# A chunked delta-rule recurrence: four levels of a triangular inverse in 32-wide blocks, and two output blocks of an MLP interleaved

## The reference

```python
def step(state, inp):                       # for each token, 8 heads, state 64x64
    r_t, w_t, k_t, v_t, a_t, b_t = inp
    sa = jnp.einsum("bhvk,bhk->bhv", state, a_t)
    state = (state * w_t[:, :, None, :] + sa[..., None] * b_t[:, :, None, :]
             + v_t[..., None] * k_t[:, :, None, :])
    return state, jnp.einsum("bhvk,bhk->bhv", state, r_t)
...
def squared_relu_mlp(h, w_up, w_down):      # 1024 -> 4096 -> 1024
    return jnp.square(jax.nn.relu(h @ w_up)) @ w_down
```

## Time and profile before

| what | value |
|---|---|
| median of 3 runs | 2743.69 us (2730.34 to 2747.26) |
| the profiled execution | 2739.59 us |
| its span | 2737.8 us |
| mean granted TensorE clock | 0.979 of full |
| PE busy | 2587.3 us (95%) |
| chunks of the recurrence, first `u` to last `u` | 396.0 to 810.6 us |

### The profile page before, as it was taken

How to read it: one execution, slowest core, us unless ns; L and a number is a source line. 1 busy time by engine, 2 the same in 40 slices (tenths; PEclk the granted TensorE clock), 3 DMA queues, 4 the chain that set the end, 5 groups by cost and what they waited for, 6 DMA issues and landing times.

```text
span 2737.8 us, 34644 instructions
## 1 busy us (share of the span) xinstructions
PE 2587.3 (95%) x13906; PEld 2140.4 (78%) x13906; DVE 1136.0 (41%) x1331; ACT 696.1 (25%) x1053; POOL 320.1 (12%) x242
## 2 busy tenths in 40 slices
PE   6999899898989999999999999977999999999998
PEld 5888688787887788888888878744778888888887
DVE  3344466666643333323333343277333332333332
ACT  4010134433321211211122122265231121112212
POOL 0000033332323200000000040043310000000000
PEclk8999999999989999999999999999999999999999
DMA  3221000000011111111111111100111111111112
GB/s 109 79 60 52 15 1 1 2 1 2 13 35 52 41 47 47 54 46 46 47 52 46 46 41 54 31 1 0 42 44 47 47 54 46 46 46 53 46 46 77
DMA packets 166311, 110.54 MB, mean 40 GB/s; under 512 B 3582, under 2 KB 163668, under 8 KB 166228
## 3 DMA queue, kind: packets, MB, share of 16 engines
q1 hardware_dynamic: 163756, 100.39, 12.3%
q0 software_dynamic: 2416, 8.91, 1.0%
q10 hardware_dynamic: 56, 0.01, 0.0%
HBM read 102.49 MB, written 6.29 MB: 40 GB/s over the span
## 4 chain that ended last, share of the span: by engine, by line
PE 83%; DVE 9%; ACT 4%; issue 3%; DVEq 0%; DMA 0%; POOL 0%; SPq 0%; ACTq 0%; POOLq 0%
PE ps L261 70%; PE ps L958 1%; PE ps L1368 1%; PE ps L961 1%; PE ps L947 1%; DVE probs L1396 1%; DVE softmax_stats L1401 1%; PE ps L913 1%; DVE mlp_lo L450 1%; DVE stage L447 1%; PE ps L975 1%; ACT stage L423 1%; PE ps L895 1%; ACT mlp_hi L425 1%; DVE x_level L1059 1%
## 5 line engine op out<-in xcount | busy, mean ns | idle before, releaser
L261 PE MATMUL ps<-h_hi,w_hi 128*128 128x512 f32 x1856 | 579.2, 393 | 23.3 <-DVE h_lo L1706 10.1
L261 PE MATMUL ps<-h_lo,w_hi 128*128 128x512 f32 x1856 | 575.6, 391 | 0.0
L261 PE MATMUL ps<-h_hi,w_lo 128*128 128x512 f32 x1856 | 574.3, 391 | 0.0
L222 ACT CAST w_hi<-w_raw 128x1024 fp32r<-128x1024 f32 x180 | 189.3, 1052 | 966.1 <-PE ps L261 966.1
L261 PEld LDWEIGHTS ps<-h_hi,w_hi 128*128 128x128 f32 x1856 | 347.8, 189 | 98.4 <-issue 14.8
L261 PEld LDWEIGHTS ps<-h_lo,w_hi 128*128 128x128 f32 x1856 | 350.8, 189 | 74.0
L261 PEld LDWEIGHTS ps<-h_hi,w_lo 128*128 128x128 f32 x1856 | 350.6, 189 | 73.8
L261 PE MATMUL ps<-mlp_hi,w_hi 128*128 128x512 f32 x1024 | 317.7, 391 | 10.7 <-DVE mlp_lo L450 10.7
L261 PE MATMUL ps<-mlp_lo,w_hi 128*128 128x512 f32 x1024 | 315.5, 389 | 0.0
L261 PE MATMUL ps<-mlp_hi,w_lo 128*128 128x512 f32 x1024 | 315.4, 389 | 0.0
L455 DVE TENSOR_TENSOR residual<-residual,ps 128x1024 f32<-128x1024 f32 x128 | 156.2, 1220 | 355.8 <-PE ps L261 355.8
(11 more groups left out here) (249 smaller groups left out, 2451.3 us busy)
## 6 DMA issues: line engine op xcount, KB each, us to landing
w_raw<-in_mlp_up SPq DMA_DIRECT2D x64, 512.0 KB, 4.0
w_raw<-in_mlp_down SPq DMA_DIRECT2D x64, 512.0 KB, 3.4
w_raw<-in_w_in_ab SPq DMA_DIRECT2D x26, 512.0 KB, 3.9
w_raw<-in_w_qkv SPq DMA_DIRECT2D x10, 512.0 KB, 3.9
x_in_tile<-in_x POOLq DMA_DIRECT2D x8, 512.0 KB, 4.2
w_raw<-in_w_out_ab SPq DMA_DIRECT2D x8, 512.0 KB, 4.1
w_raw<-in_w_o SPq DMA_DIRECT2D x8, 512.0 KB, 3.9
out<-out_chunk SPq DMA_DIRECT2D x8, 512.0 KB, 3.2
```

Source lines behind the costliest of these rows:

```text
L222: nc.scalar.copy(WH[:, slot], WR[:, slot]).then_inc(w_hi, 1)
L261: m = nc.tensor.matmul(acc(a_slot, half), ww, xx[:, k, half * HALF:(half + 1) * HALF], start=first, stop=last)
```

## The change

The first four levels keep only the 32x32 diagonal blocks, packed side by side in tiles of 128x256 (`TIC`, its transpose `TTC`, `YLC`, `MTC`). A product of a level becomes 32 matmuls of 32x32: all eight heads of diagonal tile 0, then of tile 1, and so on. There is one y and one dt for all heads, no dtt: DVE transposes the 32x32 blocks (`TTC` from `TIC`), at the start too, where this takes the place of PE's transposes and ACT's copies. POOL first copies the four diagonal quarters of `MTRB` to `MTC`, then makes `TTC`, then all four masked `XLC`; after level 3 it copies `TTC` to the diagonal of `TIT` for level 5, and ACT copies two quarters to `TI5`. DVE now waits for POOL's `tt` between the masks m and n. In the MLP the first two output blocks are interleaved.

```diff
+        def diag_products(ps, left, right):
+            for q in range(4):
+                for h in range(8):
+                    m = nc.tensor.matmul(ps[quarter(q), h], left[quarter(q), h], right[quarter(q), h],
+                                         start=True, stop=True)
+            return m
+
+        def diag_levels(t, c, s, prep, outp):
+            T, MM = solve_pe, nc.tensor.matmul
+            for k in range(MASKED):
+                solve_pool.wait(t, c, f"x{k}")
+                solve_dve.wait(t, c, f"t{k - 1}" if k else "ti")
+                T.done(diag_products(block_bank(2, 32), XLC[:, k], TIC), f"y{k}")
+                if k == 0:
+                    solve_dve.wait(t, c, "n1")
...
+                    T.done(m, "nv")
+                if outp:
+                    out_pe_step(t, c - 1, k)
+                if prep:
+                    prep_pe_step(t, c + 1, 1 - s, k)
+                solve_act.wait(t, c, f"y{k}")
+                if k:
+                    solve_dve.wait(t, c, f"tt{k - 1}")
+                T.done(diag_products(block_bank(3, 32), TTC, YLC), f"dt{k}")
...
         def chunk_act(act, c, s, prep, outp):
-            solve_pe.wait(act, c, "t0_0")
-            T.done(nc.scalar.copy(heads(TI, 0), bank(0)), "t0_0")
...
+                if k < MASKED:
+                    solve_pe.wait(act, c, f"y{k}")
+                    T.done(nc.scalar.copy(YLC[:, :], block_bank(2, 32)[:, 0:8]), f"y{k}")
+                elif k == 4:
+                    solve_dve.wait(act, c, "t3")
+                    nc.scalar.copy(TI5[quarter(0), :, 0:32], TIC[quarter(0)])
+                    T.done(nc.scalar.copy(TI5[quarter(1), :, 32:RH], TIC[quarter(1)]), "half")
...
         def chunk_dve(dve, c, s, prep, outp):
+                    solve_pool.wait(dve, c, "tt")
+                    T.done(nc.vector.transpose(TIC[:, :], TTC[:, :]), "ti")
-            for b in two:
-                T.done(TT(heads(XL, b), MTRB[:, 4 * b:4 * b + 4, 0], over(CON[:, C_MX:C_MX + P], 4), ALU.mult),
-                       f"x0_{b}")
...
+            for k in range(MASKED):
+                solve_pe.wait(dve, c, f"dt{k}")
+                T.done(TT(TIC[:, :], TIC[:, :], block_bank(3, 32)[:, 0:8], ALU.add), f"t{k}")
+                T.wait(dve, c, f"t{k}")
+                T.done(nc.vector.transpose(TTC[:, :], TIC[:, :]), f"tt{k}")
+                places(k)
...
         def chunk_pool(pool, c, s, prep, outp):
+            solve_dve.wait(pool, c, "m1")
+            for q in range(4):
+                T.done(nc.gpsimd.tensor_copy(MTC[quarter(q)], MTRB[quarter(q), :, 0, quarter(q)]), f"mc{q}")
+            T.done(TT(TTC[:, :], MTC[:, :], diag_const(C_M0), ALU.mult), "i")
+            T.done(TT(TTC[:, :], TTC[:, :], diag_const(C_I32), ALU.add), "tt")
+            for k in range(MASKED):
+                T.done(TT(XLC[:, k], MTC[:, :], diag_const(C_MX + 32 * k), ALU.mult), f"x{k}")
+            for k in range(LEVELS):
+                if k == 4:
+                    solve_dve.wait(pool, c, "tt3")
+                    for q in range(4):
+                        T.done(nc.gpsimd.tensor_copy(TIT[quarter(q), :, quarter(q)], TTC[quarter(q)]), f"full{q}")
...
         def mlp_pe(t, l):
+            def first_pair(g, after):
+                for n, (m, k) in enumerate(((0, 0), (0, 1), (0, 2), (1, 0), (1, 1), (0, 3), (1, 2), (1, 3))):
+                    if n < 3 or k == 3:
+                        t.wait_ge(act_lo, 4 * NG * l + 4 * g + 2 + k)
+                    if n == 3:
+                        t.wait_ge(acc_free[1], a0_ // 2 + 6 * g + 3)
+                    for ww, xx in ((w_h, ACh), (w_h, ACl), (w_l, ACh)):
...
+                first_pair(g, after)
+                for m in range(2, 8):
```

More of the change, by code:

```diff
@@ L295, in group @@
                             between=between if j == 0 else None)
-                for m in range(8):
+                first_pair(g, after)
+                for m in range(2, 8):
                     product(t, m // 2 % 2, m % 2, a0_ // 2 + 6 * g + 2 + m // 2, u0 + 8 * g + 4 + m // 2,
[L298 to L301, removed]
+                            GF, 256, P * (m % 2), ACh, ACl, new_unit=m % 2 == 0,
+                            between={2: lambda m=m: after(t, m - 1)} if after else None)
             group(0, norm_between(t, f"mlp{l}"))
@@ L857, in quarter_blocks @@
                 waited(t, "pe")
+                if b == 0:
+                    for h in range(8):
+                        m = MM(block_bank(1, 32)[low, h], TTC[low, h], YLC[low, h], start=True, stop=True)
+                    T.done(m, "dt4")
                 for h in range(8):
[L859 to L862, removed]
+                    m = MM(block_bank(3 * b + 2, 32)[top, h], YLC[low, h], TTC[low, h], start=True, stop=True)
                 T.done(m, f"dtt4_{b}")
@@ L867, in half_blocks @@
             top, low = slice(0, RH), slice(RH, P)
-            solve_dve.wait(t, c, "t4_0")
+            solve_dve.wait(t, c, "t4")
+            solve_act.wait(t, c, "half")
             waited(t, "pe")
@@ L879, in half_blocks @@
             solve_dve.wait(t, c, "tt4_1")
+            solve_pool.wait(t, c, "full3")
             for b in two:
@@ L918, in chunk_pe @@
                     prep_pe_step(t, c + 1, 1 - s, HEAD[1])
-            for b in two:
[L920 to L962, removed]
+            diag_levels(t, c, s, prep, outp)
+            quarter_blocks(t, c, s, prep, outp)
+            half_blocks(t, c, s, prep, outp)
             for p in range(4):
@@ L1042, in chunk_dve, with places @@
             T, TT = solve_dve, nc.vector.tensor_tensor
+            def places(k):
+                for b in two:
+                    if outp:
+                        out_dve_step(dve, c - 1, 1 - s, (k, b))
+                    if prep:
+                        prep_dve_step(dve, c + 1, 1 - s, (k, b))
             if prep:
@@ new lines, in chunk_dve @@
+            for k in range(MASKED):
[4 more added lines that the diff above has]
+                places(k)
+            q0, q1, q2, q3 = (quarter(i) for i in range(4))
+            solve_pe.wait(dve, c, "dt4")
+            T.done(nc.vector.tensor_copy(TI5[q1, :, 0:32], block_bank(1, 32)[q1, 0:8]), "t4")
@@ new lines, in chunk_dve @@
+            solve_pe.wait(dve, c, "dtt4_0")
+            T.done(nc.vector.tensor_copy(TIT[q0, :, q1], block_bank(2, 32)[q0, 0:8]), "tt4_0")
+            solve_pe.wait(dve, c, "dtt4_1")
+            T.done(nc.vector.tensor_copy(TIT[q2, :, q3], block_bank(5, 32)[q2, 0:8]), "tt4_1")
+            places(4)
+            for b in two:
+                solve_pe.wait(dve, c, f"dtt5_{b}")
+                T.done(nc.vector.tensor_copy(TIT[0:RH, 4 * b:4 * b + 4, RH:P],
+                                             block_bank(3 * b + 2, RH)[0:RH, 0:4]), f"tt5_{b}")
@@ L1090, in chunk_dve @@
+            places(5)
             solve_pe.wait(dve, c, "u")
@@ L1099, in chunk_pool, with diag_const @@
             T, TT = solve_pool, nc.gpsimd.tensor_tensor
+            def diag_const(col):
+                return over(CON[:, col:col + 32], 8)
             if prep:
```

158 lines of the change are left out of this document (83 added, 75 removed).

## The result

The changed kernel takes 2824.36 us (median of 4 runs, 2811.19 to 2829.03), the kernel before 2737.02 us on the same chip, 87 us less. The recorded ratio is 1.0297, 95% interval 1.0263 to 1.0331, that is 72 to 91 us with 81 in the middle. The ratios given are the recorded ones; they can differ by a few thousandths from the quotient of two medians, and where the text counts by ratios, it counts by these. The profiled execution took 2824.97 us, its span is 2822.8 us.

A forecast was written before the change was run, and what follows sets the result against it. PE, busy 95% of the span, was taken as the bound. To 2739.6 us it added 112 (eight chunks at +14: clock +17.5, gain 3.5), took 10 for the MLP, and added 4 to the median: 2846 us, range 2750 to 2900.

The forecast's parts named there:

- PE bounds, and an edit counts by PE's queue: Whole kernel: PE busy 95% of the span; an edit counts by PE's queue or a handover PE waits for.
- MLP, -10: MLP: interleaved output blocks remove PE's 16 waits for the last hidden block, 0.67 us each; -10 us in sum.
- A new product 1.8 us at full clock: Levels: 64 instructions at 0.0275 us each, 1.8 us, the same as an old product of eight heads.
- The head loses 1 us: Start of the levels: y0 earlier, but nv and ACT's square later behind POOL's copies and DVE's wait; 1 us lost.
- Levels at full clock, -3.5 us a chunk: Recurrence: saved third products and transposes, less open handovers, net -3.5 us a chunk, -28 for eight.
- The clock falls near y0 and comes back in the tail or behind L785 and L686: Recurrence, each chunk: clock falls near y0, returning in the tail or for a while after L785 and L686.
- Two thirds of 31 us of work low: PE's work from y0 to L981's end: 20.5 of 31 us low, less 3 hidden, +17.5 us a chunk.
- 32-wide blocks double at low, 3.7 us a product: Levels: 32-wide products take some 3.7 us at 0.50 against 1.9 at 1.00, taken from 64-wide rows.
- the second rival: Levels: a low clock doesn't slow 32-wide blocks; +3 us a chunk, 2758 us in all; chance 0.09.
- The sum: Whole kernel: +14 us a chunk, +112 for eight, MLP -10, 2842; with 4 to the median 2846 us.
- What holds the clock is work on the full array; small blocks count for little: PE's clock: full-array work holds it, small blocks count for little, like idle time.
- Fast rival, 2706: Recurrence: the clock holds, or falls only here and there, giving 2706 us; chance 0.15.

The follow-up runs named there:

- fill_full: The changed kernel plus eleven discarded 128x128 by 512-column products a chunk, ahead of y0 and behind each y and dt; 2801.84 us, ratio to before 1.0267.
- rec_alone: The changed kernel with the MLP's old loop, so the recurrence part alone; 2842.75 us, ratio to before 1.0407.
- fill_small: The changed kernel plus discarded products of 16 blocks of 32x32, three ahead of y0, one behind each y and dt; 2884.17 us, ratio to before 1.0543.
- turn_fill: The changed kernel with the four diagonal tiles taken in turn and eleven discarded full-array products a chunk; 2703.54 us, ratio to before 0.9904.
- turn_head: The changed kernel with diagonal tiles in turn, masks n0, n1 before DVE's wait for tt, and nv ahead of y0; 2715.07 us, ratio to before 0.9932.

## Why the prediction was right

The forecast was 2846 us, and 2824 came. The sign and the mechanism were right: small blocks let the clock fall, and the low clock outweighs the work saved. Of its signs all came but the 3.7 us of a product at 0.50: the clock low for 307 of the 430 us from 400 to 830, a period of 70.7 us, PE idle 3.12 us ahead of y0 by POOL, no wait on `mlp_lo`. Two terms were off in size, the MLP and the small blocks at the low clock, and one, the levels at full clock, was never measured.

- *PE bounds, and an edit counts by PE's queue*: right, 91% of the chain.
- *MLP, -10*: the wait went as said, but it was worth 15.6 us (87.04 for 88.01 us a group, 16 times). The mis-sized term is the 0.67 us a wait; 0.97 was gained. I read the matmuls' wait where the weight loads' one, 1.1 us each, bounds it from the other side.
- *A new product 1.8 us at full clock*: 1.88 with its tail. The row of 32 instructions (L847) from which I took it has this same neighbour order, and I took 27.5 ns as the cost of a small block. It is the cost of a small block behind one on the same quarter. In turn a block's instruction costs 0.75 us / 64, some 12 ns. The forecast was right only because the kernel has the order of the row. For the old product the pair that I read (L958, L961) has eight instructions in 0.99 us, so 1.98 for sixteen and not 1.8: this term of the saving was if anything too small. By the Trainium skill ("TensorE: Matmul & The Clock Gate", "Wait — 56ns, not 53.3ns?") 25 ns is the floor however small the matmul; the 12 ns here contradict it for blocks on different quarters.
- *The head loses 1 us*: not readable, since the clock falls as `nv` starts, but its parts are. y0 4.5 us behind the masks m was forecast, 4.6 came (m ends at 494.34, y0 at 498.94). PE idle 3.1 us ahead of it, by POOL, as forecast. The copies were 0.44 us each for 0.53, the products 0.72 for 0.64, the transpose 0.45 for 0.42, a handover 0.60 to 0.65 for 0.5 to 0.6.
- *Levels at full clock, -3.5 us a chunk*: not shown. No run held the clock in the order of the changed kernel; fill_full came nearest, with 208.6 us low, and its best chunks took 61.4 us with 13.7 low and eleven fillers in them, against 59.2 before.
- *The clock falls near y0 and comes back in the tail or behind L785 and L686*: just so in chunk 2, at 500.9 and 541.9. In half of the chunks the low stretch is longer, 51 to 58 us, and ends in the tail.
- *Two thirds of 31 us of work low*: this is 20.5 us of work, which doubled is 41 us low a chunk. 51 us came between the first and the last `u`: more than two thirds.
- *32-wide blocks double at low, 3.7 us a product*: 3.03, by 1.6. This term was too dear, six or seven products a chunk by 0.65 us, and the longer low time took back most of it. With the assumed -3.5, the clock costs 15.0 us a chunk (70.7 - 59.2 + 3.5), against 17.5 forecast. An estimate from the rows of chunk 2 has this size too: seven products 1.15 us longer each than the first, `nv` 1.7, L811 0.9 and L712 0.9 longer than the same shapes at 1.00 make 11.5 us, and this chunk's period grew by 9.7 (58.2 to 67.9). That they slow hardly at all, the second rival, is not so.
- *The sum*: the recurrence was forecast at +112, rec_alone gave +112 and the changed kernel's profile +99 up to the last `u`; that the first number agrees to the unit is luck, as the terms above show. Seven chunks give 80 of the 99, 11.5 each for 14 forecast; 18.4 come ahead of the first `u`, which I had counted as one more chunk.
- *What holds the clock is work on the full array; small blocks count for little*: shown, by fill_small against fill_full, for small blocks of 32x32 with 32 columns; which of these measures counts is not parted. The rule of the Trainium skill that I weighed ("TensorE: Matmul & The Clock Gate", Part 1: the clock falls after idle windows) does not cover it: 40.45 of 40.50 us busy at a clock of 0.56, with the fall behind 5 us without a gap.
- *Fast rival, 2706*: it didn't happen, since the clock fell. turn_fill, with the tiles in turn and full-array fillers, took 2703.5 and was low for 93 us; that this is near 2706 is chance, since its products cost less than the rival's.

## What to carry to other kernels

Packing a computation into small blocks saves multiplications, but here a product of small blocks takes PE hardly less time (1.88 us for 2.04), and it puts at risk a clock that everything around it needs: look up the granted clock over the stretch, and try real or discarded full-array matmuls where PE would wait. When several small blocks lie on different quarters of the array, walk over the quarters in the inner loop; the order alone was worth 73 us here. And when an engine waits for a slow neighbour, look at what stands behind the wait (n0, n1 and `nv` here), and let it pass.

## What the runs showed of the hardware that I had not expected

- 64 instructions of a 32x32 product take 1.88 us with eight neighbours on the same quarter and 0.75 to 0.87 us with the four quarters in turn, at the full clock; 3.03 and 1.08 at the low one. The same-quarter price rises by 1.6 when the clock halves, not by 2, while 16 instructions of L975's shape go from 2.00 to 3.66 us, by 1.8.
- A PE without a gap is no protection: in fill_small the clock fell behind 5 us of 32x32 blocks with no idle time, and 40.45 of 40.50 us were busy at a mean granted clock of 0.56.
- Eight discarded full-array products a chunk, 64 in the recurrence's eight, took 1.7% off turn_head (ratios 0.9932 and 0.9764, 46 us), though PE does more work. The low time went from 293 to 77 us.
